# A streaming encoder in fp32 on one core: weight sums by GpSimd, S3 in two places, the sum of squares later

## The reference, cut to what matters

```python
for l in range(DEPTH):                                     # DEPTH = 2
    x = x + 0.5 * swiglu(rmsnorm(x, ffn1_norm[l]), ...)     # (silu(x Wg) * (x Wu)) Wd, D_FF = 2816
    h = rmsnorm(x, mix_norm[l])
    x = x + (conv_mixer(h) if l % 2 == 0 else attn_mixer(h))
    x = x + 0.5 * swiglu(rmsnorm(x, ffn2_norm[l]), ...)
y = rmsnorm(x, final_norm)
```

## Time and profile before

| | us |
|---|---|
| median of 3 runs | 2232.3 (2229.56 to 2233.25) |
| profiled execution | 2228.65 |
| its span, first to last instruction | 2226.5 |
| TensorE busy | 2162.7 (97%) |
| VectorE busy | 1298.8 (58%) |
| ScalarE busy | 952.6 (43%) |
| GpSimd busy | 201.8 (9%) |
| mean granted TensorE clock | 0.991 |

### The profile page before, as it was taken

The page is one execution under the profiler, slowest core; times in us unless marked ns, Lnnn a source line. Parts: engine busy times, 40 slices in busy tenths (PEclk is TensorE's granted clock), DMA queues, the critical chain, the costliest instruction groups (busy, mean ns, idle before and its releaser), DMA issues.

```text
span 2226.5 us, 37187 instructions
## 1 busy us (share of the span) xinstructions
PE 2162.7 (97%) x15122; PEld 2050.5 (92%) x15122; DVE 1298.8 (58%) x1764; ACT 952.6 (43%) x1629; POOL 201.8 (9%) x259
## 2 busy tenths in 40 slices
PE   8899999999999999999999999999999998999997
PEld 6899999889989999998999999987787888999997
DVE  5655636668567465466655636555555466556365
ACT  5434425455445254354534525534333444345252
POOL 1101000011001010000101000000001001010000
PEclk9999999999999999999999999999999999999998
DMA  6645545466346365444745545322213146455451
GB/s 200 157 133 133 153 107 139 124 150 163 126 126 170 104 162 143 100 124 137 163 143 125 156 96 147 118 68 76 77 33 104 31 129 160 143 127 153 96 150 49
DMA packets 135416, 278.07 MB, mean 125 GB/s; under 512 B 15632, under 2 KB 20032, under 8 KB 135248
## 3 DMA queue, kind: packets, MB, share of 16 engines
q1 hardware_dynamic: 89216, 191.27, 26.4%
q0 software_dynamic: 30976, 57.53, 16.4%
q10 hardware_dynamic: 15056, 26.90, 3.5%
HBM read 268.55 MB, written 7.09 MB: 124 GB/s over the span
## 4 chain that ended last, share of the span: by engine, by line
PE 85%; DMA 5%; DVE 5%; ACT 3%; issue 2%; ACTq 0%; POOL 0%; DVEq 0%; POOLq 0%
PE ps L1346 37%; PE ps L1460 29%; PE ps L1585 8%; DMA stage<-w 5%; PE ps L1356 5%; PE ps L1565 2%; PE ps L1548 2%; ACT w_hi L629 1%; DVE w_lo L958 1%; DVE rstd L981 1%; PE ps L1534 1%; DVE stage L967 1%; DVE xa_raw L993 1%; PE ps L1363 0%; PE ps L1626 0%
## 5 line engine op out<-in xcount | busy, mean ns | idle before, releaser
L629 ACT ACTIVATE w_hi<-stage 128x1024 fp32r<-128x1024 f32 (+1 forms) x446 | 464.4, 1041 | 614.1 <-PE ps L1460 387.0
L958 DVE TENSOR_TENSOR w_lo<-stage,w_hi 128x1024 fp32r<-128x1024 f32 (+1 forms) x446 | 537.4, 1205 | 311.9 <-ACT w_hi L629 308.2
L1346 PE MATMUL ps<-xa_hi,w_hi 128*128 128x288 f32 x1280 | 381.3, 298 | 9.5 <-ACT u L671 6.4
L1460 PE MATMUL ps<-hid_hi,w_hi 128*128 128x288 f32 x1664 | 378.3, 297 | 1.8 <-DVE hid_lo L1260 1.8
L1346 PE MATMUL ps<-xb_hi,w_hi 128*128 128x288 f32 x1200 | 359.2, 299 | 20.6 <-DVE up L1022 16.8
L1346 PE MATMUL ps<-xa_lo,w_hi 128*128 128x288 f32 x1280 | 379.2, 296 | 0.0
L1346 PE MATMUL ps<-xa_hi,w_lo 128*128 128x288 f32 x1280 | 377.8, 295 | 0.0
L1460 PE MATMUL ps<-hid_lo,w_hi 128*128 128x288 f32 x1664 | 375.7, 296 | 0.0
L1460 PE MATMUL ps<-hid_hi,w_lo 128*128 128x288 f32 x1664 | 375.4, 295 | 0.0
L1346 PE MATMUL ps<-xb_lo,w_hi 128*128 128x288 f32 x1200 | 355.0, 296 | 0.0
L1346 PE MATMUL ps<-xb_hi,w_lo 128*128 128x288 f32 x1200 | 353.8, 295 | 0.0
(11 more groups left out here) (126 smaller groups left out, 2461.5 us busy)
## 6 DMA issues: line engine op xcount, KB each, us to landing
stage<-w SPq DMA_DIRECT2D x460, 256.0 KB, 3.8
stage<-w SPq DMA_DIRECT2D x104, 512.0 KB, 3.6
stage<-w POOLq DMA_DIRECT2D x200, 256.0 KB, 4.8
w_raw<-w ACTq DMA_DIRECT2D x80, 256.0 KB, 3.0
stage<-w SPq DMA_DIRECT2D x32, 384.0 KB, 3.9
k_t<-k_sb ACTq DMA_DIRECT2D x8, 288.0 KB, 2.1
v_t<-v_sb ACTq DMA_DIRECT2D x8, 288.0 KB, 2.5
y_t<-x SPq DMA_DIRECT2D x16, 144.0 KB, 1.9
```

Of the source, the lines that this page charges most:

```text
L629: act.activation(prepared(w_hi, b), raw_of(b), ACT.Copy).then_inc(w_hi_done, 1)
L958: dve.tensor_tensor(prepared(w_lo, b), raw_of(b), prepared(w_hi, b).bitcast(F32), ALU.subtract).then_inc(w_ready, 1)
L1346: mm = pe.matmul(ps[:, bank, 0:HALF], wt[:, b % W_SLOTS, w], xt[:, k, :], start=(start and k == 0 and n == 0), stop=(k == KQ - 1 and n == ...
L1460: mm = pe.matmul(ps[:, bank + i, 0:HALF], wt[:, b % W_SLOTS, w], xt[:, k, cols(h)], start=(k == 0 and n == 0), stop=(k == p.k - 1 and n == 2))
```

## The change

- S3 of groups j with j // 2 odd, in the `late` parts, is loaded into the unit of A11, which these groups don't use; the others keep S3's unit.
- The accumulating DMAs of S1 and S3 have counts of their own, one for S1 and two for S3 in each set (`pair_added` has 6 entries). A sum S2 waits for that of S3 alone, the split of S1's batch for that of S1.
- GpSimd makes S2 and S4 (`add_weights` moves from VectorE's list to GpSimd's). Its list for a phase is `add_groups`: S3 of group 0; then for each g: S1 of g, S3 of g+1, and the sums of g.
- In `late`, P6 of group 1 comes before P3 of group 0, on TensorE, ScalarE (`second_product`), VectorE and in the plan.
- The sum of squares over the partitions comes after the second product of `early` (the third in the first phase) and not after the first.

```diff
--- before.py
+++ after.py
...
@@ -189,9 +189,6 @@
         self.freed_at = {}
         for b in range(W_SLOTS, len(self.batches)):
             self.freed_at.setdefault(self.free_run[b - W_SLOTS], []).append(b)
-        self.sums_at = {}
-        for b, sums in self.sum_batch.items():
-            self.sums_at.setdefault(self.free_run[b - W_SLOTS] - 1, []).extend(sums)
 
     def start_run(self, p, kind, j):
         p.run[kind, j] = self.runs
...
@@ -237,24 +234,32 @@
         self.start_run(p, kind, j)
         base = 7 * part
         if kind == ("P1" if p.kind == "next" or j >= DT else "P6"):
-            for piece, row, second in ((S3, 2 * j, 0), (A21, 2 * j + 1, 0), (A11, 2 * j, 0), (A12, 2 * j, 1),
-                                       (A22, 2 * j + 1, 1)):
-                if piece != A11 or kind == "P1":
-                    self.load_piece(base + piece, p.row + row, second)
-            self.added[part] += 1
-            p.adds.append((part, p.row + 2 * j + 1, 16 * self.loaded[base + S3], 16 * self.loaded[base + A21]))
+            s3 = A11 if kind == "P6" and j // 2 % 2 else S3
+            p.piece["s3", j] = s3
+            pieces = [(s3, 2 * j, 0), (A21, 2 * j + 1, 0), (A12, 2 * j, 1), (A22, 2 * j + 1, 1)]
+            if kind == "P1":
+                pieces.insert(2, (A11, 2 * j, 0))
+            for piece, row, second in pieces:
+                self.load_piece(base + piece, p.row + row, second)
+            sum1, sum3 = part, 2 + 2 * part + (s3 == A11)
+            self.added[sum1] += 1
+            self.added[sum3] += 1
+            p.piece["sums", j] = {"P5": (STAGE + sum1, 16 * self.added[sum1]),
+                                  "P7": (STAGE + sum3, 16 * self.added[sum3])}
+            p.adds.append((base + A21, sum1, base + s3, sum3, p.row + 2 * j + 1, 16 * self.loaded[base + s3],
+                           16 * self.loaded[base + A21]))
+        s3 = p.piece["s3", j]
         if kind == "P6":
-            need = (32 * self.added[part], 16 * self.loaded[base + A22], 16 * self.loaded[base + A12])
-            assert all(self.split_by[base + u] <= self.splits for u in (S2, S4))
-            self.sum_batch.setdefault(len(self.batches), []).append((self.sets, part, need))
-            for u, step in ((S3, 1), (A22, 1), (A12, 2)):
+            need = (p.piece["sums", j]["P7"], 16 * self.loaded[base + A22], 16 * self.loaded[base + A12])
+            p.sums.append((self.sets, base, base + s3, need, self.split_by[base + S2], self.split_by[base + S4]))
+            for u, step in ((s3, 1), (A22, 1), (A12, 2)):
                 self.summed_by[base + u] = 2 * self.sets + step
             p.piece["set", j] = self.sets
             self.sets += 1
-        piece = PIECE_OF[kind]
+        piece = s3 if kind == "P7" else PIECE_OF[kind]
         sums = 2 * p.piece["set", j] + SUM_STEP[piece] if piece in SUM_STEP else 0
-        if piece in (S1, S3):
-            self.add_piece(p, kind, j, base + piece, 0, (STAGE + part, 32 * self.added[part]))
+        if kind in ("P5", "P7"):
+            self.add_piece(p, kind, j, base + piece, 0, p.piece["sums", j][kind])
         else:
             self.add_piece(p, kind, j, base + piece, sums)
 
...
@@ -277,9 +282,9 @@
 
 
 def late_order(n, close):
-    order = [("P6", 0), ("P7", 0), ("P5", 0), ("P3", 0)]
+    order = [("P6", 0), ("P7", 0), ("P5", 0), ("P6", 1), ("P3", 0)]
     for j in range(1, n):
-        order += [("P6", j), ("P4", j - 1), ("P5", j), ("P7", j), ("P3", j)]
+        order += [("P6", j)] * (j > 1) + [("P4", j - 1), ("P5", j), ("P7", j), ("P3", j)]
     return order + [("P4", n - 1)] * close
 
 
...
@@ -572,16 +577,38 @@
                 pool.dma_start(kc[:, t % 2, :], cache_kt[t]).then_inc(cache_loaded[t % 2], 16)
                 pool.dma_start(vc[:, t % 2, :], cache_v[t]).then_inc(cache_loaded[t % 2], 16)
 
-            def add_pairs(p):
-
-                for part, row, first_loaded, second_loaded in p.adds:
-                    base = 7 * part
-                    pool.wait_ge(raw_loaded[base + S3], first_loaded)
-                    pool.dma_start(stage[:, base + S3, :], w8[row][:, 0:PIECE], accum_op=ALU.add
-                                   ).then_inc(pair_added[part], 16)
-                    pool.wait_ge(raw_loaded[base + A21], second_loaded)
-                    pool.dma_start(stage[:, base + S1, :], w8[row][:, PIECE:2 * PIECE], accum_op=ALU.add
-                                   ).then_inc(pair_added[part], 16)
+            def add_s3(s1, sum1, s3, sum3, row, first_loaded, second_loaded):
+
+                pool.wait_ge(raw_loaded[s3], first_loaded)
+                pool.dma_start(stage[:, s3, :], w8[row][:, 0:PIECE], accum_op=ALU.add
+                               ).then_inc(pair_added[sum3], 16)
+
+            def add_s1(s1, sum1, s3, sum3, row, first_loaded, second_loaded):
+
+                pool.wait_ge(raw_loaded[s1], second_loaded)
+                pool.dma_start(stage[:, s1, :], w8[row][:, PIECE:2 * PIECE], accum_op=ALU.add
+                               ).then_inc(pair_added[sum1], 16)
+
+            def add_weights(s, base, s3, need, s2_split, s4_split):
+
+                pool.wait_ge(raw_loaded[need[0][0]], need[0][1])
+                pool.wait_ge(raw_loaded[base + A22], need[1])
+                from_count(pool, w_ready, s2_split)
+                pool.tensor_tensor(stage[:, base + S2, :], stage[:, s3, :], stage[:, base + A22, :],
+                                   ALU.add).then_inc(sum_done, 1)
+                pool.wait_ge(sum_done, 2 * s + 1)
+                pool.wait_ge(raw_loaded[base + A12], need[2])
+                from_count(pool, w_ready, s4_split)
+                pool.tensor_tensor(stage[:, base + S4, :], stage[:, base + S2, :], stage[:, base + A12, :],
+                                   ALU.add).then_inc(sum_done, 1)
+
+            def add_groups(p):
+                add_s3(*p.adds[0])
+                for g in range(len(p.adds)):
+                    add_s1(*p.adds[g])
+                    if g + 1 < len(p.adds):
+                        add_s3(*p.adds[g + 1])
+                    add_weights(*p.sums[g])
 
             def attention_inputs():
                 pool.wait_ge(hid_ready, MIXER.hidden)
...
@@ -600,7 +627,7 @@
 
             for p in PHASES:
                 if p.kind in ("first", "next", "conv"):
-                    add_pairs(p)
+                    add_groups(p)
                 if p.source == "conv":
                     pool.wait_ge(state_kept, DT)
                     pool.dma_start(conv_out_state, state_out[:, :, :]).then_inc(state_stored, 16)
...
@@ -714,15 +741,22 @@
                         act.wait_ge(c12_done, p.c11s + j + 1)
                         seed(p, j + 2, est[:, j + 2, HALF:TOK])
 
-                for j in range(p.n):
+                def second_product(j):
                     take_u2(p, j)
                     split_hi(p.run["P6", j])
+
+                second_product(0)
+                for j in range(p.n):
+                    if j > 1:
+                        second_product(j)
                     if j == 0:
                         split_hi(p.run["P7", j])
                     else:
                         split_hi(p.run["P4", j - 1])
                     take_u4(p, j)
                     split_hi(p.run["P5", j])
+                    if j == 0:
+                        second_product(1)
                     if j > 0:
                         split_hi(p.run["P7", j])
                         if p.kind == "first":
...
@@ -957,19 +991,6 @@
                         dve.wait_ge(w_hi_done, PLAN.batches[b].ready)
                         dve.tensor_tensor(prepared(w_lo, b), raw_of(b), prepared(w_hi, b).bitcast(F32),
                                           ALU.subtract).then_inc(w_ready, 1)
-                for s, part, need in PLAN.sums_at.get(run, ()):
-                    add_weights(s, part, need)
-
-            def add_weights(s, part, need):
-                base = 7 * part
-                dve.wait_ge(pair_added[part], need[0])
-                dve.wait_ge(raw_loaded[base + A22], need[1])
-                dve.tensor_tensor(stage[:, base + S2, :], stage[:, base + S3, :], stage[:, base + A22, :],
-                                  ALU.add).then_inc(sum_done, 1)
-                dve.wait_ge(sum_done, 2 * s + 1)
-                dve.wait_ge(raw_loaded[base + A12], need[2])
-                dve.tensor_tensor(stage[:, base + S4, :], stage[:, base + S2, :], stage[:, base + A12, :],
-                                  ALU.add).then_inc(sum_done, 1)
 
             def add_square(n, i, c):
                 dve.wait_ge(sq_done, squares_before(n) + i + 2 + (DT if n == 0 else 0))
...
@@ -1075,8 +1096,10 @@
             def late(p):
                 if p.kind == "conv":
                     dve.memset(ue[:, :, 0:CONV_PAD], 0.0)
+                split_lo(p.run["P6", 0])
                 for j in range(p.n):
-                    split_lo(p.run["P6", j])
+                    if j > 1:
```

(9 more changed lines are left out.)

6 lines of the change are left out of this document (3 added, 3 removed).

## The result

The changed kernel takes 2272.14 us in the median (2271.68 to 2275.53) against 2231.92 for the kernel before, measured beside it (2229.56 to 2233.25), four runs each: ratio 1.0185, 95% interval 1.0167 to 1.0202. It is 40 us slower where no change was forecast, and outside the range of 2216 to 2254.

The account below looks back on a forecast made before the run. TensorE, busy 97% of the span, was taken as the bound, with only about 64 us idle. Terms -6.4 + 0 + 5.8 + 1.0 = +0.4 us gave 2233 us, no change; range 2216 to 2254.

Parts of the forecast that it names:

- the sums on GpSimd: Late-part loop: sums on GpSimd use up what S3 and S1 gave; three groups 29.2 us against 27.7, together 0.
- `next`: Phases where S3 keeps one place: late sums stall P5; with the gate part of `conv`, 5.8 us lost.
- The sum of squares: Five TensorE waits after a part's first product vanish, 5.6 us plus 0.8 of pipe refilling: -6.4 us, nothing taking it back.
- P6 of group 1: Late parts: moved ahead of P3 of group 0, starts A22's load for group 3 1.9 us earlier; no gain of its own.
- S3 in two places, separate counts: Late parts: sum S2 no longer waits for S1's DMA; something for even groups, nothing for odd, used up by GpSimd's sums.
- A22 alone is left, its unit freed by the same split as before: Late parts: S2 would wait only for A22's load, released as before, so odd groups gain nothing.
- A: Length of one GpSimd addition over 512 columns: 1.2 us, with bounds 0.52 and 1.38.
- Landing to sum: Late-part loop: from A22's landing to the finished sum, 2.93 us on GpSimd against 0.79 before.
- Lock: Rival: GpSimd and VectorE keep each other out, 7.5 us in late parts, 12 in `next`, giving 2252; chance 0.24.
- The slack argument: Even groups of `next`: sums arrive with slack between -0.4 and +0.3 us for P5; 2.3 us of stalls, plus refills.
- Clock: A low-clock stall in the fourth FFN's late part goes or shrinks, others come at P4 of group 2: +1 us.
- My rival for it: Stalls in five late parts pull the clock down, 2 us each: +10, giving 2242; chance 0.10.

Follow-up runs that it names:

- the S3 kernel: Kernel before with only S3 in two places and the DMAs adding to S1 and S3 counted apart, sums on VectorE: 2207.90 us, ratio 0.9911.
- short additions: Changed kernel with each GpSimd addition cut to 32 of its 512 columns, waits and order kept: 2220.68 us, ratio 0.9962.
- memsets: Changed kernel with each of GpSimd's two additions replaced by a memset of the same 128x512 target, order kept: 2225.59 us, ratio 0.9987.
- the exchange: Changed kernel with GpSimd's two additions of group g ahead of the DMA adding to S3 of group g+1: 2223.87 us, ratio 0.9969.

## Why the prediction was wrong

The step that failed is the price of the sums on GpSimd: 0 in the late parts and 5.8 us in `next` and the gates, against before. Measured are 26.8 and 19.1 us. It is taken apart below, behind the smaller terms. (What the prediction calls the third FFN, with the stretch at 660 and 783 us, is the second; it is the third late part.)

**The sum of squares (forecast -6.4).** The wait went as told, one of 4.2 us is left. "Here I find nothing that takes the gain back" was wrong: the waits for `take_u4` went from 6.4 to 9.2 us and those for `take_c22` from 16.8 to 17.8. By first products the `early` parts are 6.8 us shorter and the late parts 5.1 longer. My reading is that they wait for the loop of loads, which doesn't start earlier; I had written that very reason for P6 of group 1 and not applied it here. Where the loop is shorter (on top of the S3 part) the median falls by 3.4 us against before; the intervals of those two kernels overlap, so that this remainder is not shown.

**P6 of group 1 (forecast 0).** Alone -5.4; on top of the other two -4.1, with overlapping intervals, so that there it isn't shown.

**S3 in two places, separate counts (forecast: something for even groups, taken back by the sums).** Measured 21 us with the sums on VectorE; this is the largest error on the fast side. The step of it that failed is "A22 alone is left, its unit freed by the same split as before ... the odd ones nothing". The landing that I held fixed moved: in the third late part of the S3 kernel,

```profile
680.29 1.23 DVE L976 TENSOR_TENSOR w_lo<-stage,w_hi 128x1024 fp32r<-128x1024 f32 x1
...
684.51 0.69 DVE L984 TENSOR_TENSOR stage<-stage 128x512 f32<-128x512 f32 x1 [0.47 <-DMA stage<-w]
```

S2 starts 2.99 us after the split that freed A22's unit ended, where before A22 alone took 4.71 from that split. This is the most favourable place. Over the middle groups of the five late parts, S2 starts 3.1 us after the issue of A22's load in odd groups (3.5 before) and 5.6 us after it in even ones (6.5 before). So the odd groups won 0.4 us where I had nothing. The even ones won 1.0, although A22 itself took longer to land there (5.3 us from its issue, 3.8 before): of the 3.4 us from its landing to the end of S2, 1.0 were left, since S1 no longer counts. What makes a load land sooner or later, no run isolates.

**The sums on GpSimd (forecast 0 in the late parts, with the gains of S3 in it; 5.8 in `next` and the gates).** This is the step that decides: the sums cost 69 us against the kernel with them on VectorE. For the third late part I had 15.3 to the sum of group 3, 29.2 to that of group 6, 2.8 to P4 and 24.3 for the rest, 71.6; measured are 17.5, 31.3, 2.9 and 24.1, 75.7. In the mean of the five parts the first two are 17.3 and 30.7, and a part lasts 77.1.
- *Length.* A was 1.2, bounds 0.52 to 1.38. The shortest additions take 1264 ns (L602), the usual one right behind a DMA issue is recorded as 1.61, which is the 1.6 that I had named as a sign of being wrong. From the start of the issue to the end of S2 it is 2.17 us (221.59 to 223.76), where I had 0.75 + 1.2. So A was 0.2 us short on each link. The larger fault is that its price was set off against gains of S3 whose size I never wrote down.
- *Order.* Right in kind: S2 does wait behind S3 of g+1. Landing to sum was to be 2.93 us; it is 3.1 in the mean. In the even-to-odd link of the chain above it is 4.7, and the link 12.0 us against 11.0, as S3 lands 2.2 us behind A22 there (721.08 and 718.87) and not the 0.7 that I took. The order alone costs 20 us (short additions) to 25 us (memsets).
- *Lock.* It stood outside the sum, as a rival at 0.24 with 19.5 us: 7.5 in the late parts, where only the 5.2 us of stretched VectorE work in `conv` is found, and 12 in `next`, where with the gates 19 us were lost to lock and length. A meeting costs up to the whole of the other's instruction (2.43 for 0.76), on both engines: GpSimd's additions in the first `early` part took 1.88 to 2.27 us. The Trainium skill (SBUF — State Buffer, section "SBUF: two separate sides") has the pair of ports locked for a whole instruction when VectorE has two SBUF inputs and GpSimd reads SBUF; the runs agree: 2.43 us beside an addition, 0.76 beside memsets, and no change for VectorE's operations that read PSUM.
- *Against the lock* I had set that "in the late parts VectorE sits idle before a sum". For the late parts that held in the changed kernel too. In `next` the order put S2 at the moment of `make_hidden`, as the exchange showed.

So the 69 us (70 between the profiled spans) are, by the table of stages: order some 18 us and length some 29 in the late parts, lock and length together 19 in `next` and the gates, and 4 in the first `early` part, where VectorE's operations of 1.35 us were stretched to 2.3 to 2.95. How the 19 us divide isn't shown. By the medians the order is 25, and length and lock are 44. The table gives the late parts' share of it to length, because the lock would have to show in durations there and doesn't; whether a longer addition costs by S2 itself or by holding back GpSimd's next issues, no run separates.

**`next` (forecast +5.8 with the gates of `conv`).** +14.6 in `next` and +4.6 in the gates, against the sums on VectorE. The places were right: 16 of the 26 waits for `take_u2` are in `next`, each before P5, and take 9.1 us without the refilling of the pipe. The slack argument was right too. In all 16 the addition S2 itself is not stretched (1.60 to 1.62 us). Two things were short: the 0.2 us of A, and GpSimd's issue, which comes some 0.9 us later than in the kernel with memsets (for the fourth S3 of the long `next` phases, 36.7 us after their start against 35.8, in the mean of four). That it is late because `make_hidden` holds up VectorE's splits, which free the units, is my reading. With memsets, S2 also ends 0.8 us sooner, and no wait is left. The two kernels with short additions and with memsets lose under 1 us in `next`, so that here the order costs nothing by itself.

**Clock (forecast +1).** The mean granted clock fell from 0.991 to 0.985; with the sums on VectorE it is 0.994. Two windows around the wait of 2.21 us that ends at 726.41:

```profile
722.00:726.00 4.00, 2.21 (x17) 1.97 (x15) 1.25 (x2) 2.31 (x5) 3.62 (x4) 1.00 0.47 66
726.00:730.00 4.00, 3.59 (x16) 3.59 (x17) 3.01 (x4) 1.61 (x4) 0.00 (x0) 0.57 0.83 204
```

After it the granted clock is 0.57 of full, mostly the lower level, 1.2 GHz. Of the 7440 matmuls on L1370, 198 start 0.2 to 0.35 us after the one before, not 0.13 (85 before, 47 with the sums on VectorE); over 0.13 that is 22 us (10 and 6). So about 16 us of the 70.5 between the spans come this way, and are in the stages above. The low stretches follow waits, so I read them as a multiplier on the stalls and not as a cause of their own; no run holds the clock fixed. My rival for it had 10.

**The sum.** Forecast -6.4 + 0 + 5.8 + 1.0. Measured by stage, clock included: early parts -2.6, late parts +26.8, `next` and gates +19.1. By cause: -28.7 for what is not the sums (I had -6.4), +69 for them. Two errors of opposite sign; without the one on the fast side the time would have been further out still.

## What to carry to other kernels

Before an operation moves to another engine, ask whether it stands in a loop on which the bottleneck engine waits. Here the length of the additions and their place behind a load, in a loop of the late parts, were two thirds of the loss, though GpSimd was 9% busy before. Then price every meeting of a GpSimd addition with a VectorE operation that reads two SBUF tiles at the length of the other instruction, and look which operation stands there in the new order. In an engine's own list, put what releases another engine ahead of what waits for a later load; here that exchange was worth 46 us. When a change consists of parts, try each without the others: 29 us were won by the parts that looked idle, and hidden by the one that looked like relief.

## What the hardware showed unexpectedly

- A VectorE operation with two SBUF inputs and a GpSimd addition exclude each other nearly whole: 0.76 became 2.43 us, and additions of 1.26 became 2.27. At that place VectorE's record starts 0.19 us before the addition's, and it is VectorE that waits. GpSimd's memsets of the same tile (675 ns) did nothing of the kind.
- GpSimd's memset of 128x512 takes 675 ns in the mean, in the other kernel 801 right behind a DMA issue and 526 behind a memset; my line through 204 and 98 ns gave 0.52, which is what it takes behind a memset.
- VectorE's operations with PSUM inputs (L1043) kept their 452 ns (at most 459) beside GpSimd's additions.
